# Attention: the query chunks of a head in another order, with the rotary key rounded once and a late norm

## What is computed

```python
q = (rms_norm(c_q, q_norm_g) @ w_uq).reshape(B, S, MLA_HEADS, MLA_NOPE + MLA_ROPE)
kv = (rms_norm(c_kv, kv_norm_g) @ w_ukv).reshape(B, S, MLA_HEADS, MLA_NOPE + MLA_V)
k_rope = rope(k_r, cos, sin)
s = jnp.einsum('bqhd,bkhd->bhqk', qn, k_nope) + jnp.einsum('bqhr,bkr->bhqk', qr, k_rope)
mask = key_chunk[None, :] <= q_chunk[:, None]
p = jax.nn.softmax(jnp.where(mask, s, -jnp.inf), axis=-1).astype(v.dtype)
return jnp.einsum('bhqk,bkhd->bqhd', p, v)
```

## Time and profile before

| | us |
|---|---|
| median of three runs | 2363.5 (2359.74 to 2364.39) |
| span of the profiled execution | 2362.4 |
| attention stage in it, first matmul to last output | 583.5 to 1231.6 |
| PE, DVE, ACT, POOL busy over the span | 2161.9, 1648.6, 1239.8, 448.0 |

### The profile page before, as it was taken

The page is one execution under the profiler, slowest core; times in us unless marked ns, Lnnn a source line. Parts: engine busy times, 40 slices in busy tenths (PEclk is TensorE's granted clock), DMA queues, the critical chain, the costliest instruction groups (busy, mean ns, idle before and its releaser), DMA issues. The chain is left out here.

```text
span 2362.4 us, 40869 instructions
## 1 busy us (share of the span) xinstructions
PE 2161.9 (92%) x13164; PEld 1830.6 (77%) x13165; DVE 1648.6 (70%) x3080; ACT 1239.8 (52%) x2127; POOL 448.0 (19%) x257
## 2 busy tenths in 40 slices
PE   7999999999799998999989999499999999999970
PEld 7888899898577777777877888378888888888850
DVE  5444444465777878778775877778898876777746
ACT  5333333323566666766763221167676755655637
POOL 0000000000100000000001111124443543435426
PEclk9999999999899999999999999599999999999985
DMA  4111111343000000000025333489999988878837
GB/s 184 64 63 62 62 62 65 125 136 121 4 7 6 18 6 8 15 5 12 7 82 184 142 142 124 176 327 367 358 377 375 362 289 280 302 276 280 296 77 279
DMA packets 83216, 361.87 MB, mean 153 GB/s; under 512 B 25808, under 2 KB 37840, under 8 KB 68112
## 3 DMA queue, kind: packets, MB, share of 16 engines
q1 hardware_dynamic: 70144, 318.88, 35.7%
q0 software_dynamic: 11520, 41.16, 7.2%
q10 hardware_dynamic: 1440, 0.37, 0.1%
HBM read 291.97 MB, written 68.94 MB: 153 GB/s over the span
## 5 line engine op out<-in xcount | busy, mean ns | idle before, releaser
L2356 DVE TENSOR_TENSOR w_raw<-w_raw,w_hi 128x2048 fp32r<-128x2048 f32 x128 | 286.9, 2283 | 0.0
L1172 POOL TENSOR_TENSOR qT_lo<-q_raw,qT_hi 128x512 fp32r<-128x512 f32 x32 | 40.9, 1277 | 1141.5 <-ACT qT_hi L1116 1141.5
L1134 ACT CAST prT_hi<-pT 128x512 fp32r<-128x512 f32 (+1 forms) x288 | 162.3, 564 | 145.9 <-PE pT L1038 144.6
L1254 DVE TENSOR_TENSOR prT_lo<-pT,prT_hi 128x512 fp32r<-128x512 f32 (+1 forms) x288 | 188.3, 656 | 56.5 <-ACT prT_hi L1134 54.4
L2146 PE MATMUL eH<-w_hi,at_tok 128*128 128x512 f32 x512 | 207.0, 404 | 1.7 <-DVE at_tok L2349 1.7
L2147 PE MATMUL eH<-w_hi,at_tok 128*128 128x512 f32 x512 | 204.2, 399 | 0.0
L1245 DVE TENSOR_REDUCE mx<-pS 128x1 f32<-128x512 f32 (+2 forms) x320 | 191.2, 608 | 13.4 <-PE pS L1028 6.8
L1126 ACT ACTIVATE pr<-pS,nmx 128x512 f32<-128x512 f32 (+1 forms) x240 | 151.0, 639 | 36.4 <-DVE nmx L1249 36.1
L98 POOL TENSOR_TENSOR cell<-cell 128x1 f32<-128x1 f32 x66 | 78.1, 1183 | 446.6 <-ACT y L2274 177.2
L1038 PE MATMUL pT<-ident,pr 128*128 128x128 f32 x832 | 151.3, 274 | 12.4 <-DVE prT_lo L1254 10.5
L2262 ACT CAST w_hi<-w_raw 128x2048 fp32r<-128x2048 f32 x64 | 122.5, 1915 | 74.9 <-issue 43.1
(11 more groups left out here) (434 smaller groups left out, 6088.9 us busy)
## 6 DMA issues: line engine op xcount, KB each, us to landing
w_raw<-in_w SPq DMA_DIRECT2D x96, 2048.0 KB, 12.0
xt<-in_x SPq DMA_DIRECT2D x9, 1024.0 KB, 8.3
xs<-in_x SPq DMA_DIRECT2D x8, 1024.0 KB, 5.1
scratch_h<-hp SPq DMA_DIRECT2D x16, 512.0 KB, 2.7
scratch_z<-hp SPq DMA_DIRECT2D x16, 512.0 KB, 3.6
fz<-scratch_z SPq DMA_DIRECT2D x16, 512.0 KB, 6.8
out<-fz SPq DMA_DIRECT2D x16, 512.0 KB, 2.6
scratch_xT<-xT_hi SPq DMA_DIRECT2D x7, 1024.0 KB, 4.0
```

The source lines that it names most:

```text
L1134: nc.scalar.copy(ph[:, u % RING, 0:w], T[u % NTB][:, 0:w]).then_inc(t_hi, 1)
L1254: v.tensor_tensor(pl[:, u % RING, 0:w], T[u % NTB][:, 0:w], ph[:, u % RING, 0:w].bitcast(F32), ALU.subtract).then_inc(t_lo, 1)
L2356: v.tensor_tensor(w.words(side)[:, at], w.words(side)[:, at].bitcast(F32), w.hi[:, at].bitcast(F32), ALU.subtract).then_inc(w.lo_ready if ...
```

## The change

- The order of q within every head becomes 4, 5, 0, 1, 6, 7, 2, 3 (`CHUNKS`), the same in all heads.
- The prologue holds k0, the first q chunk (the third by position), k1 and k2; v0 comes in the first step. Query chunks are projected two chunks ahead rather than three. Two value projections of the next pair stand one step earlier.
- The rotary key is rounded once, on partitions 64 to 127 of slot 0; SP copies high part and remainder to slots 1 and 2 with four DMAs, and heads 1 and 3 wait for them.
- The norm of the last span goes behind the first step's second half on DVE; the memset goes to POOL.
- PE waits for a key chunk at the first piece that reads it.

```diff
@@ -797,8 +797,8 @@
-HEAD_STEPS = [list(range(NQ)) if h % 2 == 0 else list(range(NQ))[::-1] for h in range(HEADS)]
-STEPS_B = [(h, q) for h in range(HEADS) for q in HEAD_STEPS[h]]
+CHUNKS = (2, 0, 3, 1)
+STEPS_B = [(h, 2 * c + x) for h in range(HEADS) for c in CHUNKS for x in range(2)]
@@ -813,16 +813,15 @@
-PROLOGUE = [("k", 0, 0), ("q", 0, 0), ("v", 0, 0), ("q", 0, 1)]
-FIRST_STEPS = {(0, 0): [("k", 0, 1)], (0, 1): [("v", 0, 1), ("q", 0, 2)], (1, 0): [("k", 0, 2)], (1, 1): [("v", 0, 2)],
+PROLOGUE = [("k", 0, 0), q_chunk(0), ("k", 0, 1), ("k", 0, 2)]
+FIRST_STEPS = {(0, 0): [("v", 0, 0)], (0, 1): [q_chunk(1)], (1, 0): [("v", 0, 1)], (1, 1): [("v", 0, 2)],
                (2, 0): [("k", 0, 3)], (2, 1): [("v", 0, 3)]}
-V_STEPS = {(3, 0): 0, (4, 1): 1, (6, 1): 2, (7, 0): 3}
+V_STEPS = {(2, 1): 0, (3, 1): 1, (6, 1): 2, (7, 0): 3}
@@ -834,8 +833,8 @@
-    if i == 1 and n % 2 == 1 and n // 2 + 3 < NQC:
-        out.append(q_chunk(n // 2 + 3))
+    if i == 1 and n % 2 == 1 and n // 2 + 2 < NQC:
+        out.append(q_chunk(n // 2 + 2))
@@ -947,6 +946,11 @@
+                sp.wait_ge(rope_copied, 4)
+                sp.wait_ge(rope_lo, 4)
+                for slot in (1, 2):
+                    for k in (kh, kl):
+                        sp.dma_start(k[0:64, slot].bitcast(F32), k[64:128, 0].bitcast(F32)).then_inc(rope_again, 16)
@@ -973,8 +977,7 @@
-                        pe.wait_ge(rope_copied, 2 * e + 2)
-                        pe.wait_ge(rope_lo, 2 * e + 2)
+                        pe.wait_ge(rope_lo, e + 1)
@@ -1014,13 +1017,14 @@
-                        if h == 3:
-                            pe.wait_ge(rope_again, 2)
-                        pe.wait_ge(k_copied, K_AT[PREP_NO["k", h - x, q // 2] + 1])
-                        pe.wait_ge(k_lo, K_AT[PREP_NO["k", h - x, q // 2] + 1])
-                        pe.wait_ge(q_hi, n // 2 + 1)
+                        if h in (1, 3) and n % NQ == 0:
+                            pe.wait_ge(rope_again, 32 if h == 1 else 64)
                         pe.wait_ge(q_lo, n // 2 + 1)
                     for j in range(PIECES[n][i]):
+                        made = K_AT[PREP_NO["k", h - x, j] + 1]
+                        if made > keys_seen[0]:
+                            keys_seen[0] = made
+                            pe.wait_ge(k_lo, made)
@@ -1086,9 +1090,7 @@
-                    for x in range(2):
-                        half = slice(64 - 64 * x, 128 - 64 * x)
-                        nc.scalar.copy(kh[half, x, c * 512:(c + 1) * 512], S[c][half, :]).then_inc(rope_copied, 1)
+                    nc.scalar.copy(kh[64:128, 0, c * 512:(c + 1) * 512], S[c][64:128, :]).then_inc(rope_copied, 1)
@@ -1141,8 +1143,8 @@
-                    if p[0] == "q":
-                        round_q(p)
+                    if m == 2:
+                        round_q(PROLOGUE[1])
@@ -1166,15 +1168,10 @@
+                nc.gpsimd.memset(rsum[:], 0.0).then_inc(cleared, 1)
-                    if no == 3:
-                        pool.wait_ge(rope_copied, 8)
-                        pool.wait_ge(rope_lo, 8)
-                        nc.gpsimd.tensor_copy(kh[0:64, 2], kh[0:64, 1]).then_inc(rope_again, 1)
-                        nc.gpsimd.tensor_copy(kl[0:64, 2], kl[0:64, 1]).then_inc(rope_again, 1)
@@ -1286,6 +1283,8 @@
                                 ready(p)
+                            if (n, i) == (0, 1):
+                                late_norm()
```

More of the change, by code:

```diff
@@ L814, in q_chunk @@
 def q_chunk(s):
-    h, c = s // 4, s % 4
-    return ("q", h, c if h % 2 == 0 else 3 - c)
+    return ("q", s // 4, CHUNKS[s % 4])
 NQC = 4 * HEADS
 QRING = 4
-PROLOGUE = [("k", 0, 0), ("q", 0, 0), ("v", 0, 0), ("q", 0, 1)]
-FIRST_STEPS = {(0, 0): [("k", 0, 1)], (0, 1): [("v", 0, 1), ("q", 0, 2)], (1, 0): [("k", 0, 2)], (1, 1): [("v", 0, 2)],
+PROLOGUE = [("k", 0, 0), q_chunk(0), ("k", 0, 1), ("k", 0, 2)]
+FIRST_STEPS = {(0, 0): [("v", 0, 0)], (0, 1): [q_chunk(1)], (1, 0): [("v", 0, 1)], (1, 1): [("v", 0, 2)],
                (2, 0): [("k", 0, 3)], (2, 1): [("v", 0, 3)]}
-V_STEPS = {(3, 0): 0, (4, 1): 1, (6, 1): 2, (7, 0): 3}
+V_STEPS = {(2, 1): 0, (3, 1): 1, (6, 1): 2, (7, 0): 3}
 def prep_in(n, i):
@@ L906, in phase_b @@
         O = [psum(f"pO{i}") for i in range(2)]
-        w_loaded = [sem("w_loaded0"), sem("w_loaded1")]; folded = sem("folded"); late = sem("late_span"); rope_copied = sem("rope_copied"); rope_again = sem("rope_again"); rope_lo = sem("rope_lo")
+        w_loaded = [sem("w_loaded0"), sem("w_loaded1")]; folded = sem("folded"); late = sem("late_span"); rope_copied = sem("rope_copied"); rope_again = sem("rope_again"); keys_seen = [0]; rope_lo = sem("rope_lo")
         k_lo = sem("k_lo"); q_hi = sem("q_hi"); q_lo = sem("q_lo")
@@ L922, in chunk_no @@
         def chunk_no(p):
-            return 4 * p[1] + (p[2] if p[1] % 2 == 0 else 3 - p[2])
+            return 4 * p[1] + CHUNKS.index(p[2])
         def probs(n, i):
@@ L1185, in rope_rest, with late_norm @@
                 def rope_rest(c):
[L1186 to L1189, removed]
+                    keys = slice(c * 512, (c + 1) * 512)
+                    v.wait_ge(rope_copied, c + 1)
+                    v.tensor_tensor(kl[64:128, 0, keys], S[c][64:128, :], kh[64:128, 0, keys].bitcast(F32), ALU.subtract).then_inc(rope_lo, 1)
                 for c in range(4):
                     rope_rest(c)
[L1192 to L1198, removed]
+                def late_norm():
+                    v.reciprocal(root, root).then_inc(late, 1)
+                    v.wait_ge(late, 2)
+                    v.scalar_tensor_tensor(t["ckvn"][:, at], t["late_raw"][:, 0, :], t["gkv"][:, 0:1], root[:, 0, :], ALU.mult, ALU.mult).then_inc(late, 1)
+                    for n in range(2):
+                        v.scalar_tensor_tensor(t["cqn"][:, n, at], t["late_raw"][:, 1 + n, :], t["gq"][:, n:n + 1], root[:, 1, :],
+                                               ALU.mult, ALU.mult).then_inc(late, 1)
                 def rope(p):
```

## The result

The changed kernel takes 2376.84 us (median of four runs, 2375.02 to 2381.91) where the kernel before takes 2363.26 in the same count; the ratio is 1.0061 (95% interval 1.0049 to 1.0073). The forecast was 2378. The profiled execution has a span of 2373.2 us, 10.8 over the one before. But its stage of attention starts 2.8 us earlier (580.7 against 583.5), in code that the change does not touch, so the stage itself grew from 648.1 to 662.1 us: +14.0, where the sum said +14.3.

A forecast was written before the change was run, and what follows sets the result against it. No engine full, TensorE nearest; score pieces stall on a loop of maximum, exponential and four banks. Terms -1.8 + 25.2 - 7.2 - 1.7 + 0.2 + 1.5 - 1.9 = +14.3 us give 2378, range 2352 to 2391.

The forecast's parts named there:

- The starved step: q6 of every head, with one unit between its four-piece tiles, and the wait into q7: 25.2 us added.
- The K and V term: Next pair's projections in odd heads, K on q4, q0, q6 and q2 with less cover in two: +1.5 us.
- The short steps q0 and q1: Short steps of neighbouring heads no longer meet: 2.0 us gained at each of three meetings, 1.2 in the last head, -7.2.
- The start: Stage's first steps: first score 5.5 us earlier, a hole behind the late norm, possible half clock; -1.8 us in sum.
- The end: Last step with its drain: q3 leaves four units, 2.6 us lost against 4.5 before; -1.9 us.
- No half clock inside the stage: Sign expected in the attention stage: TensorE's granted clock does not fall to half; no size given.
- The -1.7 us for head 2: Clock fall at the first meeting of short steps goes away; head 2 took 69.4 us against head 4's 67.7: -1.7.
- Rival 3: Each starved q6 drops the clock; eight falls would give some +12 to +13 us, 2390; chance 0.08.
- The copies by SP: Four 512 KB DMAs of the rotary key, read by head 1 some 75 us behind the first score: hidden, priced nothing.
- 1: Rival: q6 tiles' waits overlap as in their old place, 25.2 us falls away, -10.9 remains, 2353; chance 0.2.
- 2: Rival: half of that cover, later pieces finding banks from the short step: +1.7 us, 2365, no measurable change; chance 0.17.
- Rival 4: The start loses: late norm's 4.8 us wholly on top, half clock through step 1; 2385 with the forecast's steps; chance 0.08.

The follow-up runs named there:

- the order-only run: Changed kernel with the new order, prologue and look-ahead alone, rotary key, late norm and copies as before: 2378.49 us, ratio 1.0066 to the kernel before.
- the run with the order in head 0 alone: Changed kernel with the new order in head 0 only, heads 1 to 7 up and down as before: 2362.78 us, ratio 0.9999 to the kernel before.
- the run with the projection in it: Changed kernel with the query projection from the end of q1 put between the two tiles of q6: 2386.99 us, ratio 1.0104 to the kernel before.
- the run with the start parts alone: Kernel before plus rotary key rounded once and copied by SP, late norm behind the first step, memset on POOL; old order: 2359.99 us, ratio 0.9991.
- the run with the late rounding: Changed kernel with the query chunk's rounding on ScalarE behind the tile's last exponential, not its first: 2377.36 us, ratio 1.0056 to the kernel before.

## Why the prediction was right, and where its terms were off

- **The starved step, 25.2 us forecast.** An even q6 stalls 3.6 us (10.6 less 7.0), and the q7 behind it 0.7 more than before: 4.3, where 4.4 was said for both. This term was right; the second tile was reckoned 0.5 too slow, and the wait into q7 a little too short. An odd q6 stalls 6.5 (14.3 less 7.8 with the key projection), since key and value projections stand in and before it. In q6's windows alone, against 1.8 and 0.6 before, that is 4 x 1.8 + 3 x 5.9 + 3.0 (the last head has neither projection), 27.9. The mechanism, its place and its engine are what the trace, the order-only run and the run with the order in head 0 alone show. (By the forecast's own numbers the odd term is 4.4 - 0.6 = 3.8, not 3.7.)
- **The K and V term, 1.5 us**, was too small and is inside the 27.9 above: moving either out of q6 shortened it by 1.1 to 1.6 us.
- **The steps of a middle pair** (table above). The forecast's terms give 6.3 - 2.0 + 0.05 + 0.5, some +4.8 us, the windows +4.1. The single terms are further off. q6 and q7 together lose 7.1 us more than before, where 6.3 + 0.5 less 1.1 for the odd q7 is 5.7. The short steps q0 and q1 gain 1.6, where 2.0 was said: the even head's do as well as forecast, the odd head's hold key and value projections. And q2 to q5, for which the forecast's remarks add up to a loss of about 1.1, gain 1.4, most of it in q2 and q3 together (-1.3). The misses of 1.4 and 2.5 offset each other.
- **The start, -1.8 us.** The first score came 11.1 us after the first matmul, not 11.4. The hole behind the late norm was 4.58 us, where about 5 was said; the clock fell for 3.4 us right behind it, and for 3.4 us in the first step. The third step began at 37.5 us after the first matmul, where 39.5 was said. But the 4.0 us more of PE work that the forecast credits to that point are too many. By its own prices it is about 1.7, because the kernel before has by then (38.8 us after its first matmul) issued one query projection, one key and one value projection more. So the start gained about 3.0 us (38.8 - 37.5 + 1.7); with the right work and its own times the forecast would have been a loss of 0.5. Here too two errors offset each other.
- **The end, -1.9 us.** The last step took 15.0 us for about 12.1 of work (the 6.3 of before, four units and 2.1 of score pieces more): 2.9 lost against 4.5, so -1.6.
- **By pairs of heads** the forecast's terms read +4.0, +3.1, +4.8 and +2.2; with the moved work taken out the windows read +3.1, +4.0, +4.1 and +2.8. No pair is off by more than 1 us, but the total, +14.3 against +14.0, is closer than the terms it is made of, and that much is luck.
- **The clock.** "No half clock inside the stage" was wrong. It fell in three of four odd heads in or just behind q6, for 3.4 us each; in one it fell on the dense q7 behind, which took 17.1 us in place of 15.5, in two others inside the waiting, where the step was no longer than the one without a fall. The -1.7 us for head 2 was thus half right: the fall at 773 us is gone, and one in head 3 takes 1.6 back. Altogether 17.1 us of the stage are at half clock in both kernels. Rival 3 is so far real, but at 1.6 us and not 12. The rule of the Trainium skill that I set beside it ("TensorE: Matmul & The Clock Gate", section "HAM oscillation — how this bites in real kernels") is borne out in kind by the falls in and behind the odd q6; that it should come with each hole is not, since all four even q6 kept 1.00.
- **The copies by SP** landed within 8.8 us of their issue at 585.8 to 589.0, some 79 us ahead of their first reader (head 1, at 676.5); no wait on them shows. The answer of the changed kernel's trace for that line (issues, us from issue to landing, what waits for them):

```profile
L953 SPq DMA_DIRECT2D kT_hi<-kT_hi x2: 553/1230/1906, 585.8 to 587.1; - x2
L953 SPq DMA_DIRECT2D kT_lo<-kT_lo x2: 587/1506/2424, 586.4 to 589.0; - x2
...
DMA to landing us min/median/max: 4.3/7.2/8.8
```

- **The rivals.** 1 and 2 rested on cover and parted from the forecast at a stall of about 2.7 us per q6; with 3.6 in the even heads and 6.5 in the odd ones neither holds. Nor can the hole be filled at will: the run with the projection in it shows this. Rival 4, a start that loses, is ruled out by the run with the start parts alone.

What stays open: about 1 us of the odd q6, why the clock falls in an odd q6 of one head and not of another, and how much of the differences between runs of one kernel is where its falls come to lie. That the same code behind the stage took 1129.1 to 1135.0 us says that single effects of a few us can't be read from one total.

## What to carry to other kernels

Where a tile's last piece releases its first (a maximum before any exponential), look for the step whose tile takes all the buffers, and count the independent work between two such tiles; it must be as long as the loop from last piece to first free buffer (here 2.3 us), or each tile pays the rest. Part of the wait lies in the next step, so price both together. A new order of steps moves this work from one step to the next, so pair each step with the units of its predecessor before anything else, and check that no work crossed the borders of the windows that you compare. And work of the waiting engine is no filler if its result needs the same buffers and the engines that the loop runs through.

## What was not expected of the hardware

- The granted clock fell to half for 3.4 us at different places from kernel to kernel, in steps that are otherwise alike to 0.1 us: in the run with the late rounding at 1014.3 in a q5, in the changed kernel in or behind q6. A fall cost 1.6 to 1.9 us when dense work lay under it (17.1 against 15.5; 14.4 against 12.5) and close to nothing inside a wait (an odd q6 took 14.3 us with and without).
- Four copies of 512 KB between partitions of SBUF, issued one behind the other, landed in 4.3 to 8.8 us each. That is less than the 12.0 us of a 2048 KB load, but more than a quarter of it.
